# Three of eight groups of X per layer scaled on ScalarE and turned plainly, LN sums with operands added on VectorE over more units, V products 256 wide

## The chip, the core and the metric

The kernel runs on one core of one Trainium2 chip, and the metric is the time of that core in microseconds. The core has TensorE (PE, matmul; its weight loads are PEld), VectorE (DVE), ScalarE (ACT), GpSimd (POOL) and SyncE (SP), which here only issues transfers. Each engine carries out its own list of instructions in order; they meet through semaphores.

## The reference

One block of attention and MLP (first block, one layer) and then two layers of a second block, on 256 tokens of width 2048, all in float32. Cut to what the change touches:

```python
def one_block(args):                       # first block, attention, 16 heads of 128
    ...
    a = jnp.where(mask, jnp.exp(log_beta + suffix), 0.0)
    return jnp.einsum('bhqk,bhkd->bhqd', a.astype(v.dtype), v)      # the V products
...
for l in range(DEPTH_2):                   # second block, two layers
    h = rms_norm_2(x, norm_g[l]) * (1.0 + scale) + shift
    z = h @ w_in[l]                        # 2048 x 4928
    ...                                    # attention (mla), and beside it:
    u = causal_depthwise_conv(u, dw_w[l], dw_b[l])                  # 31 taps, 1024 channels
    u = jax.nn.silu(layer_norm(u, conv_ln_g[l], conv_ln_b[l]))      # mean and variance over channels
    u = u @ w_pw[l] + b_pw[l]
    conv_out = u * jax.nn.silu(conv_gate)
    y = jnp.concatenate([mla_out, conv_out], axis=-1) @ w_out[l]
    x = x + gate * y
```

## The kernel before

All products with weights are cut into units. A unit is a block of weights of 128 x 1024 numbers (one transfer of 512 KB) and the matmuls that use it: for each of two blocks of 128 weight rows and each of two tiles `t` of 128 tokens, three matmuls 512 wide (high part times high, high times low, low times high of a float32 split in two), 12 in all. `after[n]` lists the small tasks of step `n`. Each engine walks over the steps and carries out its part of the tasks of `after[n]`; TensorE does it behind unit `n`, ScalarE and VectorE do it ahead of the weights of that step. ScalarE makes the high part `WH` of a unit's weights (`high`, L1187), VectorE the low part `WL` (L1218); a step of both normally prepares the unit four further on, and ScalarE waits there until the unit four back has left its buffer. TensorE starts a unit when `WL` of it is written. So a task that comes late on VectorE holds up everything that stands behind it in its list.

I call the first unit of a layer's product with `w_in` z0. Tasks that the change touches:

- **Start of a layer (`chain`, L288).** x is kept with tokens on the partitions, in X[128, t, 2048]; z needs it turned, with channels on the partitions, and scaled by 1/rms of the token. Per layer there are 8 groups of 4 blocks of 128 x 128, named (t, q). `h_turn` (L591) turns a group and scales it at once, by a float32 matmul of each block of X with a diagonal matrix DG that holds 1/rms. `h_shift` (ScalarE, L997) or `h_scale` (VectorE, L1387) then applies the column's factor and shift and writes FB, four instructions 128 wide a group; `h_split` rounds it to the high part on ScalarE (L984) and takes the low part on VectorE (L1218, `AHL<-FB,AHL`). Groups (0, 3), (1, 2), (1, 3) come last: TensorE turns them behind z0+1, z0+2 and z0+3. The first eight units need the groups one after another: z0+6 is the first that reads group (1, 3), in its fourth matmul, which waits for that low part (`rows`, L784).
- **V products (`sb_out`, L578).** For each of 16 heads three float32 matmuls 128 wide: V0 with two blocks of TA, and V1 with one.
- **Layer norm of the convolution (L385 on).** The convolution ends on VectorE at step z0+96. Then `ln_sum` adds channel tiles (VectorE), `ln_mean` sums over the partitions with a matrix of ones (TensorE, three float32 matmuls 256 wide, L667), `ln_centre` takes the mean off (VectorE), squares (ScalarE, L1122) and adds pairs of squares (VectorE, L1565, L1567), `ln_var` sums these over the partitions (TensorE, four float32 matmuls one column wide, L675), `ln_rstd` (VectorE and POOL), `ln_scale` multiplies (VectorE, L1578), and `ln_act` does four pairs cp of channel tiles: silu (ScalarE, L1129), high part ULH (ScalarE, L1133), low part ULL (VectorE, L1218, `ULL<-SQL,ULH`). These feed the product with `w_pw`, whose first unit is z0+108; unit z0+108+cp waits for ULL of pair cp.
- **`o_add` (L1604).** Between them stands the product with the upper half of `w_out`, units z0+92 to z0+107. Its column block c is added to x on VectorE by four instructions 512 wide (L1612, L1613, L1617 twice), in the lists of steps z0+95, z0+99, z0+103 and z0+107.

All of this is one list per engine written out in Python; there is no scheduler. `ln_act` of the last pair is put ahead of the other tasks of its step:

```python
for cp in range(4):
    after[s + 7 + cp].insert(0 if cp == 3 else len(after[s + 7 + cp]), ("ln_act", l, cp))   # s = z0 + 97
```

Of the kernel before, what the change touches and what calls it, by code (L numbers as in the profile page):

```python
# [9 lines left out]
ALU = mybir.AluOpType  # L10
# [70 lines left out]
def build(nc, A, out):  # L81
    ctx = ExitStack()
    with ctx:
# [97 lines left out]
        U1 = put("U1", [128, 2, 512], off=oBH + 4 * K)  # L181
        DG = put("DG", [128, 2, 128], off=oBH)
# [242 lines left out]
        for c in range(4):  # L425
# [33 lines left out]
        rope_zero = tally("rope_rows_cleared")  # L459
# [6 lines left out]
                   kr_sq, kr_ms, kr_rot, q_sq, q_ms, q_rstd, q_rot, rot, k_sq, k_ms, k_rs, k_nrm, k_rope, rope_zero, mx, ex, rcp, o_high, conv_d, x_mid, p_bias, p_gated,  # L466
# [8 lines left out]

        flat = lambda ap: ap.rearrange("p a b -> p (a b)")
# [15 lines left out]
        def tensor_program(e):  # L492
# [354 lines left out]
        def scalar_program(e):  # L847
# [333 lines left out]
            def high(n):  # L1181
# [3 lines left out]
                if n >= NH:  # L1185
# [4 lines left out]
                         sb_scores=sb_scores, sb_high=sb_high, sb_sums=sb_sums, sb_out=sb_out, hid_evict=hid_evict, hid_split=hid_split, h_split=h_split, h_first=h_first, h_shift=h_shift, x_end_square=x_end_square, high=high,  # L1190
# [22 lines left out]
        def vector_program(e):  # L1213
# [201 lines left out]
            def pads_(l):  # L1415
                e.wait_ge(*T.ready(("h", l, 7)))
# [132 lines left out]
            def ln_sum(l, part):  # L1549
                for ct in range(4 * part, 4 * part + 4):  # L1550
                    e.wait_ge(*conv_d.at(l, ct, 30))
                if part == 0:
                    over_tiles(FB[:, 2, 0:256], CA[:, 0:4, :]).then_inc(*ln_d.up(l, "sum", 0))
                else:
                    e.tensor_tensor(FB[:, 3, :], flat(CA[:, 4:6, :]), flat(CA[:, 6:8, :]), ALU.add).then_inc(*ln_d.up(l, "sum", 1))

            def ln_centre(l):
# [9 lines left out]
                e.tensor_tensor(SQL[:, 0, :], SQL[:, 0, :], SQL[:, 2, :], ALU.add).then_inc(*ln_d.up(l, "squares"))  # L1567
# [36 lines left out]
            def o_add(l, part, c):  # L1604
# [10 lines left out]
                for t in range(2):  # L1615
# [6 lines left out]
                         att_scores=att_scores, att_recip=att_recip, att_out=att_out, att_back=att_back, conv=conv, ln_sum=ln_sum, ln_centre=ln_centre,  # L1622
# [231 lines left out]
```

## Time and profile before

| | |
|---|---|
| median of three runs | 1913.95 us (1913.6 to 1915.55) |
| the profiled execution | 1914.18 us, of which the span of the trace is 1912.3 us |
| PE busy | 1905.0 us, 100% of the span, 9406 instructions |
| PEld | 1609.9 us, 84% |
| DVE | 1558.5 us, 81% |
| ACT | 1027.4 us, 54% |
| POOL | 137.0 us, 7% |
| granted TensorE clock | 1.000 over the span |
| moved by DMA | 445.22 MB, 233 GB/s |

Busy means that some instruction of the engine has its record open. Records of TensorE overlap: one 512 wide is some 390 ns long, while the next starts some 230 ns later. So a busy TensorE can still lose time, and what a matmul costs is the distance between starts (in the chain of waits, its share), not the length of its record. A float32 matmul has two records in the trace, a transpose one.

### The profile page before, as it was taken

The page shows a single profiled execution, that of the slowest core. Times are in us where ns is not written, and L with a number is a line of the kernel's source. Part 1 is how long each engine was busy: PE and PEld are TensorE (multiplying, and loading weights), DVE is VectorE, ACT ScalarE, POOL GpSimd, SP SyncE. Part 2 cuts the span into 40 slices and gives each one's busy share as a digit, 9 for nine tenths or more (in the row PEclk, how much of TensorE's full clock was granted, in tenths as well). Part 3 has the DMA queues.
Part 4 walks back from the last instruction along what each step waited for, and adds up shares of the span by engine and source line. Part 5 has one row for each costly group of instructions (what it writes and reads, how often), then busy time and mean ns, then how long its engine had stood idle before and what let it go on. Part 6 is the DMA issues. An engine that isn't in the chain of part 4 may idle for free.

```text
span 1912.3 us, 25289 instructions
## 1 busy us (share of the span) xinstructions
PE 1905.0 (100%) x9406; PEld 1609.9 (84%) x9406; DVE 1558.5 (81%) x2131; ACT 1027.4 (54%) x1509; POOL 137.0 (7%) x88
## 2 busy tenths in 40 slices
PE   9999999999999999999999999999999999999999
PEld 7888888888888888888888888888888888888887
DVE  5888888788888888888887568888898688888986
ACT  6646556454444444444445454567656555667562
POOL 1232233000000000000000000001100000010000
PEclk9999999999999999999999999999999999999999
DMA  7787877889898888888887546655556466555554
GB/s 260 248 273 252 295 248 247 272 277 313 285 302 286 294 302 284 303 296 296 284 305 253 182 154 188 192 162 166 162 188 198 144 193 177 172 168 160 200 186 143
DMA packets 259181, 445.22 MB, mean 233 GB/s; under 512 B 15883, under 2 KB 123421, under 8 KB 258803
## 3 DMA queue, kind: packets, MB, share of 16 engines
q1 hardware_dynamic: 258643, 443.42, 71.4%
q8 instruction: 75, 1.23, 0.3%
q14 instruction: 47, 0.39, 0.1%
q10 hardware_dynamic: 416, 0.19, 0.0%
HBM read 441.39 MB, written 2.16 MB: 232 GB/s over the span
## 4 chain that ended last, share of the span: by engine, by line
PE 99%; DVE 0%; ACT 0%; issue 0%; POOL 0%; ACTq 0%; DVEq 0%
PE P L741 72%; PE P L799 13%; PE P L800 6%; PE P L501 2%; PE P L595 1%; PE P L634 1%; PE P L633 1%; PE P L619 0%; PE P L561 0%; PE P L541 0%; PE P L540 0%; PE P L641 0%; PE P L726 0%; PE P L586 0%; PE P L587 0%; PE P L652 0%
## 5 line engine op out<-in xcount | busy, mean ns | idle before, releaser
L1218 DVE TENSOR_TENSOR WL<-RAW,WH 128x1024 fp32r<-128x1024 f32 (+1 forms) x649 | 790.4, 1223 | 233.9 <-ACT WH L1187 231.3
L1187 ACT ACTIVATE WH<-RAW 128x1024 fp32r<-128x1024 f32 (+1 forms) x647 | 669.8, 1046 | 520.3 <-PE P L741 252.3
L741 PE MATMUL P<-WH,AHL 128*128 128x512 f32 (+1 forms) x2048 | 642.6, 389 | 0.9 <-ACT WH L1187 0.6
L741 PEld LDWEIGHTS P<-WH,AHL 128*128 128x128 f32 x2048 | 382.1, 188 | 76.9 <-issue 1.9
L741 PE MATMUL P<-WL,AHL 128*128 128x512 f32 (+1 forms) x1024 | 392.1, 385 | 0.0
L799 PE MATMUL P<-AHL,WH 128*128 128x512 f32 x1024 | 359.9, 398 | 0.0
L741 PE MATMUL P<-WH,BH 128*128 128x512 f32 x896 | 351.4, 392 | 0.0
L741 PE MATMUL P<-WH,BL 128*128 128x512 f32 x896 | 349.0, 390 | 0.0
L741 PE MATMUL P<-WL,BH 128*128 128x512 f32 x896 | 348.8, 389 | 0.0
L800 PE MATMUL P<-AHL,WL 128*128 128x256 f32 x1024 | 282.3, 281 | 0.0
L1215 DVE SCALAR_TENSOR_TENSOR ADA<-RAW,CC,ADA 128x1024 f32<-128x1024 f32 x180 | 237.9, 1322 | 0.0
L799 PEld LDWEIGHTS P<-AHL,WH 128*128 128x128 f32 x1024 | 190.7, 188 | 44.2
L741 PEld LDWEIGHTS P<-WL,AHL 128*128 128x128 f32 x1024 | 192.4, 188 | 35.6 <-DVE WL L1218 0.4
L1215 DVE SCALAR_TENSOR_TENSOR CA<-UT,DW,CA 128x256 f32<-128x256 f32 x480 | 204.1, 476 | 0.0
L741 PEld LDWEIGHTS P<-WH,BL 128*128 128x128 f32 x896 | 168.2, 188 | 35.3
L741 PEld LDWEIGHTS P<-WL,BH 128*128 128x128 f32 x896 | 168.3, 188 | 34.4
L741 PEld LDWEIGHTS P<-WH,BH 128*128 128x128 f32 x896 | 168.2, 188 | 34.3
L800 PEld LDWEIGHTS P<-AHL,WL 128*128 128x128 f32 x1024 | 193.4, 189 | 3.1
L1662 POOL TENSOR_TENSOR ST<-ST,CST 128x4 f32<-128x4 f32 (+3 forms) x36 | 66.0, 1834 | 1504.2 <-DVE ST L1215 911.7
L1215 DVE SCALAR_TENSOR_TENSOR X<-P,ST,X 128x512 f32<-128x512 f32 x64 | 45.1, 746 | 6.9 <-PE P L741 6.7
L974 ACT ACTIVATE HID<-P 128x512 f32<-128x512 f32 x32 | 19.1, 597 | 46.8 <-PE P L799 46.8
L1366 DVE TENSOR_TENSOR HID<-P,HID 128x512 f32<-128x512 f32 x32 | 22.1, 691 | 24.1 <-ACT HID L974 24.1
(268 smaller groups left out, 1451.4 us busy)
## 6 DMA issues: line engine op xcount, KB each, us to landing
RAW<-in_ada_w_dram SPq DMA_DIRECT2D x192, 512.0 KB, 5.0
RAW<-in_mlp_w_in_dram SPq DMA_DIRECT2D x128, 512.0 KB, 4.8
RAW<-in_mlp_w_out_dram SPq DMA_DIRECT2D x128, 512.0 KB, 5.2
RAW<-in_sb_w_qkv_dram SPq DMA_DIRECT2D x95, 512.0 KB, 4.9
RAW<-in_w_in_dram SPq DMA_DIRECT2D x80, 512.0 KB, 4.0
RAW<-in_w_in_dram SPq DMA_DIRECT2D x128, 256.0 KB, 3.2
RAW<-in_w_out_dram SPq DMA_DIRECT2D x64, 512.0 KB, 4.3
RAW<-in_sb_w_o_dram SPq DMA_DIRECT2D x32, 512.0 KB, 5.3
```

The lines of the kernel that those rows point to most:

```text
L501: m = e.transpose(pb[:, (2 * i + t) * 128:(2 * i + t + 1) * 128], src[:, t, kt * 128:(kt + 1) * 128], IDN)
L595: m = e.matmul(pb[:, k * 128:(k + 1) * 128], X[:, t, (4 * q + k) * 128:(4 * q + k + 1) * 128], DG[:, t, :], start=True, stop=True)
L633: e.matmul(pb[:, o:o + n], TT[:, 0, qs], TT[:, 1, ks], start=True, stop=False)
L634: m = e.matmul(pb[:, o:o + n], TT[:, 2, t * 128:(t + 1) * 128], TT[:, 3, ks], start=False, stop=True)
L741: return e.matmul(P[:, 2 * u.pair + t, 0:u.w], x, w, start=u.first and k == 0 and part == 0, stop=u.last and k == u.nk - 1 and part == 2)
L799: both = lambda: e.matmul(o.rearrange("p (x n) -> p x n", x=2), WH[:, s, w], AHL[:, :, kt, :], start=u.first and k == 0, stop=last, skip_g ...
L800: lower = lambda: e.matmul(o[:, 0:256], WL[:, s, w], AH[:, kt, :], start=False, stop=False, skip_group_check=True)
L1187: e.activation(WH[:, n % NH, 0:size], RAW[:, i % NR, 0:size], ACT.Copy).then_inc(w_high, 1)
L1215: return e.scalar_tensor_tensor(out=o, in0=x, scalar=s, in1=y, op0=op0, op1=op1)
L1218: return e.tensor_tensor(o, x, h.bitcast(F32), ALU.subtract)
L1366: e.tensor_tensor(v, P[:, p:p + 2, 0:256], HID[:, c % 2, :, :], ALU.add).then_inc(pair_emptied[opened["m1", c][0]], 1)
L1662: return e.tensor_tensor(o, x, MH.to_broadcast([128, n]), ALU.pow)
```

## The change

X of groups (0, 3), (1, 2) and (1, 3) is multiplied by 1/rms on ScalarE into a new tile XS, as task `x_scale` at the head of steps z0, z0+1 and z0+2, and TensorE turns XS with plain transposes. After `ln_sum` VectorE adds the three operands of the mean to one in two more instructions, so that `ln_mean` is one matmul; the adding of squares is a task of its own, `ln_pairs`, one step later and with one instruction more, so that `ln_var` is two matmuls; `ln_var`, `ln_rstd`, `ln_scale` and `ln_act` come one step later. In the V products V0 meets both blocks of TA in one matmul 256 wide.

```diff
+        XS = put("XS", [128, 3, 512], off=oS)
...
-            after[b] += [("h_split", l, 1, 1)]
-            after[b + 1] += [("h_shift", l, 0, 2), ("h_split", l, 0, 2), ("h_turn", l, 0, 3)]
-            after[b + 2] += [("h_turn", l, 1, 2), ("h_shift", l, 0, 3), ("h_split", l, 1, 2)]
+            after[b] += [("x_scale", l, 0, 3), ("h_split", l, 1, 1)]
+            after[b + 1] += [("x_scale", l, 1, 2), ("h_shift", l, 0, 2), ("h_split", l, 0, 2), ("h_turn", l, 0, 3)]
+            after[b + 2] += [("x_scale", l, 1, 3), ("h_turn", l, 1, 2), ("h_shift", l, 0, 3), ("h_split", l, 1, 2)]
...
-            after[s + 5].append(("ln_var", l))
-            after[s + 5].insert(0, ("ln_rstd", l))
-            after[s + 7].append(("ln_scale", l))
+            after[s + 3].append(("ln_pairs", l))
+            after[s + 6].append(("ln_var", l))
+            after[s + 6].insert(0, ("ln_rstd", l))
+            after[s + 8].append(("ln_scale", l))
             for cp in range(4):
-                after[s + 7 + cp].insert(0 if cp == 3 else len(after[s + 7 + cp]), ("ln_act", l, cp))
+                after[s + 8 + cp].insert(0 if cp == 3 else len(after[s + 8 + cp]), ("ln_act", l, cp))
...
-                    e.matmul(o[:, 0:128], v0, TA[:, h, 0:128], start=True, stop=True)
-                    e.matmul(o[:, 128:256], v0, TA[:, h, 128:256], start=True, stop=False)
-                    m = e.matmul(o[:, 128:256], v1, TA[:, h, 256:384], start=False, stop=True)
+                    e.matmul(o, v0, TA[:, h, 0:256], start=True, stop=False, skip_group_check=True)
+                    m = e.matmul(o[:, 128:256], v1, TA[:, h, 256:384], start=False, stop=True, skip_group_check=True)
...
             def h_turn(l, t, q):
                 pb = bank(("h", l, t, q))
+                if (t, q) in scaled_slot:
+                    e.wait_ge(*x_scaled.at(l, t, q))
+                    for k in range(4):
+                        m = e.transpose(pb[:, k * 128:(k + 1) * 128], XS[:, scaled_slot[t, q], k * 128:(k + 1) * 128], IDN)
+                    m.then_inc(*T.filled(("h", l, t, q)))
+                    return
...
             def ln_mean(l):
                 pb = bank(("lnm", l))
-                for part in range(2):
-                    e.wait_ge(*ln_d.at(l, "sum", part))
-                for i, x in enumerate((FB[:, 2, 0:256], FB[:, 3, 0:256], FB[:, 3, 256:512])):
-                    m = e.matmul(pb[:, 0:256], ONE, x, start=i == 0, stop=i == 2)
+                e.wait_ge(*ln_d.at(l, "sum", 3))
+                e.matmul(pb[:, 0:256], ONE, FB[:, 2, 0:256], start=True, stop=True).then_inc(*T.filled(("lnm", l)))
...
-                for part in range(2):
-                    for t in range(2):
-                        m = e.matmul(pb[:, t:t + 1], SQL[:, 0, part * 256 + t * 128:part * 256 + (t + 1) * 128], ONE[:, 0:1],
+                for t in range(2):
+                    m = e.matmul(pb[:, t:t + 1], SQL[:, 0, t * 128:(t + 1) * 128], ONE[:, 0:1], start=t == 0, stop=t == 1, skip_group_check=True)
...
+            def x_scale(l, t, q):
+                e.wait_ge(*rstd.at(("ob", 0) if l else ("m2", 7), t))
+                e.activation(XS[:, scaled_slot[t, q], :], X[:, t, 512 * q:512 * q + 512], ACT.Copy, scale=ST[:, 74 + t:75 + t]).then_inc(*x_scaled.up(l, t, q))
...
+                    e.tensor_tensor(FB[:, 2, 0:256], FB[:, 2, 0:256], FB[:, 3, 0:256], ALU.add).then_inc(*ln_d.up(l, "sum", 2))
+                    e.wait_ge(*ln_d.at(l, "sum", 2))
+                    e.tensor_tensor(FB[:, 2, 0:256], FB[:, 2, 0:256], FB[:, 3, 256:512], ALU.add).then_inc(*ln_d.up(l, "sum", 3))
...
+            def ln_pairs(l):
                 for i in range(2):
                     e.wait_ge(*ln_a.at(l, 2 * i + 1))
                     e.tensor_tensor(SQL[:, 2 * i, :], SQL[:, 2 * i, :], SQL[:, 2 * i + 1, :], ALU.add).then_inc(*ln_d.up(l, "pair", i))
                 e.wait_ge(*ln_d.at(l, "pair", 1))
-                e.tensor_tensor(SQL[:, 0, :], SQL[:, 0, :], SQL[:, 2, :], ALU.add).then_inc(*ln_d.up(l, "squares"))
+                e.tensor_tensor(SQL[:, 0, :], SQL[:, 0, :], SQL[:, 2, :], ALU.add).then_inc(*ln_d.up(l, "quarter"))
+                e.wait_ge(*ln_d.at(l, "quarter"))
+                e.tensor_tensor(SQL[:, 0, 0:256], SQL[:, 0, 0:256], SQL[:, 0, 256:512], ALU.add).then_inc(*ln_d.up(l, "squares"))
```

`pads` (VectorE, L1416) now waits for the turning of group (1, 3). The lists of the engines move at these places.

On ScalarE, steps z0-1 to z0+3 of layer 0, before (AHL is the high part of a group, FB the shifted group, WH the weights):

```order
L997 ACTIVATE FB<-P,MOD,SCL 128x128 x4
L984 ACTIVATE AHL<-FB 128x4x128
L1187 ACTIVATE WH<-RAW 128x1024
L997 ACTIVATE FB<-P,MOD,SCL 128x128 x4
L984 ACTIVATE AHL<-FB 128x4x128
L1187 ACTIVATE WH<-RAW 128x1024
L997 ACTIVATE FB<-P,MOD,SCL 128x128 x4
L984 ACTIVATE AHL<-FB 128x4x128
L1187 ACTIVATE WH<-RAW 128x1024 x2
```

and in the changed kernel:

```order
L1004 ACTIVATE FB<-P,MOD,SCL 128x128 x4
L995 ACTIVATE XS<-X,ST 128x512
L987 ACTIVATE AHL<-FB 128x4x128
L1194 ACTIVATE WH<-RAW 128x1024
L995 ACTIVATE XS<-X,ST 128x512
L1004 ACTIVATE FB<-P,MOD,SCL 128x128 x4
L987 ACTIVATE AHL<-FB 128x4x128
L1194 ACTIVATE WH<-RAW 128x1024
L995 ACTIVATE XS<-X,ST 128x512
L1004 ACTIVATE FB<-P,MOD,SCL 128x128 x4
L987 ACTIVATE AHL<-FB 128x4x128
L1194 ACTIVATE WH<-RAW 128x1024 x2
```

Nothing is taken out here; two XS now stand ahead of the second WH (that of z0+4), and a third ahead of the last group.

On VectorE, steps z0+97 to z0+103 of layer 0, before (CA is the convolution's result, SQL the squares, G the gate row of `o_add`):

```order
L1555 TENSOR_TENSOR FB<-CA 128x512
L1218 TENSOR_TENSOR WL<-RAW,WH 128x1024 x2
L1612 TENSOR_TENSOR FB<-P,G 128x512
L1613 TENSOR_TENSOR FB<-P,G 128x512
L1617 TENSOR_TENSOR X<-X,FB 128x512 x2
L1215 SCALAR_TENSOR_TENSOR CA<-P,CA 128x1024 x2
L1565 TENSOR_TENSOR SQL<-SQL 128x512 x2
L1567 TENSOR_TENSOR SQL<-SQL 128x512
L1218 TENSOR_TENSOR WL<-RAW,WH 128x1024 x3
L1571 TENSOR_SCALAR ST<-P 128x2
```

and in the changed kernel, from the centring (CA) on:

```order
L1222 SCALAR_TENSOR_TENSOR CA<-P,CA 128x1024 x2
L1225 TENSOR_TENSOR WL<-RAW,WH 128x1024
L1579 TENSOR_TENSOR SQL<-SQL 128x512 x2
L1581 TENSOR_TENSOR SQL<-SQL 128x512
L1583 TENSOR_TENSOR SQL<-SQL 128x256
L1225 TENSOR_TENSOR WL<-RAW,WH 128x1024 x3
L1587 TENSOR_SCALAR ST<-P 128x2
L1628 TENSOR_TENSOR FB<-P,G 128x512
```

One WL is now ahead of the sums of squares, there is a fourth sum, and the WL that stood behind the small L1571 is now ahead of its counterpart L1587. Two instructions 128x256 also follow the counterpart of L1555.

On VectorE, steps z0+105 to z0+108, where ULL is the low part of a pair, before:

```order
L1218 TENSOR_TENSOR ULL<-SQL,ULH 128x512
L1218 TENSOR_TENSOR WL<-RAW,WH 128x1024
L1218 TENSOR_TENSOR ULL<-SQL,ULH 128x512
L1218 TENSOR_TENSOR WL<-RAW,WH 128x1024
L1218 TENSOR_TENSOR ULL<-SQL,ULH 128x512
L1612 TENSOR_TENSOR FB<-P,G 128x512
L1613 TENSOR_TENSOR FB<-P,G 128x512
L1617 TENSOR_TENSOR X<-X,FB 128x512 x2
L1218 TENSOR_TENSOR WL<-RAW,WH 128x1024 x4
```

and in the changed kernel:

```order
L1225 TENSOR_TENSOR ULL<-SQL,ULH 128x512
L1225 TENSOR_TENSOR WL<-RAW,WH 128x1024
L1628 TENSOR_TENSOR FB<-P,G 128x512
L1629 TENSOR_TENSOR FB<-P,G 128x512
L1633 TENSOR_TENSOR X<-X,FB 128x512 x2
L1225 TENSOR_TENSOR ULL<-SQL,ULH 128x512
L1225 TENSOR_TENSOR WL<-RAW,WH 128x1024
L1225 TENSOR_TENSOR ULL<-SQL,ULH 128x512
L1225 TENSOR_TENSOR WL<-RAW,WH 128x1024 x3
```

The first ULL in both lists is that of pair 1. The four instructions of `o_add` stood behind the ULL of pair 3; now they stand ahead of the ULL of pair 2.

## Rows read from the trace of the kernel before

**Rows 1.** The page's chain that ended last: shares by engine.

```profile
PE 99%; DVE 0%; ACT 0%; issue 0%; POOL 0%; ACTq 0%; DVEq 0%
```

**Rows 2.** Groups of TensorE by form: busy us, mean ns of one record.

```profile
L595 PE MATMUL P<-DG,X 128*128 128x128 f32 x128 | 16.4, 276 | 1.1 <-DVE DG L1384 1.0
L501 PE MATMUL P<-CST,U 128*128 128x128 f32 x64 | 8.3, 272 | 0.0
```

**Rows 3.** The chain of waits in order of time: start us, us, what, records.

```profile
108.06 0.22 PE P L586 x2
...
1133.12 0.89 PE P L595 x8
...
1137.67 2.75 PE P L741 x12
...
1204.88 0.44 PE P L501 x4
...
1424.81 1.29 PE P L667 x6
...
1434.29 0.79 PE P L675 x8
```

**Rows 4.** Timeline of ScalarE, start of layer 0: start us, us, what, [idle before].

```profile
1136.51 0.63 ACT L984 ACTIVATE AHL<-FB 128x512 fp32r<-128x512 f32 x1
1137.05 1.04 ACT L1187 ACTIVATE WH<-RAW 128x1024 fp32r<-128x1024 f32 x1
1137.99 1.49 ACT L997 ACTIVATE FB<-P,MOD,SCL 128x128 f32<-128x128 f32 x4
...
1140.05 1.04 ACT L1187 ACTIVATE WH<-RAW 128x1024 fp32r<-128x1024 f32 x1
...
1143.66 0.63 ACT L984 ACTIVATE AHL<-FB 128x512 fp32r<-128x512 f32 x1 [1.18 <-DVE FB L1387]
```

**Rows 5.** Timeline of VectorE, start of layer 0.

```profile
1141.13 1.22 DVE L1218 TENSOR_TENSOR WL<-RAW,WH 128x1024 fp32r<-128x1024 f32 x1 [0.25 <-ACT WH L1187]
...
1150.22 0.69 DVE L1218 TENSOR_TENSOR AHL<-FB,AHL 128x512 fp32r<-128x512 f32 x1 [0.70 <-ACT AHL L984]
```

**Rows 6.** Timeline of TensorE, both layers, around the fourth matmul of z0+6.

```profile
1150.01 0.62 PE L741 MATMUL P<-WH,AHL 128*128 128x512 f32 x2
...
1150.68 0.78 PE L741 MATMUL P<-WH,AHL 128*128 128x512 f32 x2
...
1542.14 0.84 PE L741 MATMUL P<-WH,AHL 128*128 128x512 f32 x2
```

**Rows 7.** Timeline of ScalarE, first attention: a 512 wide pass read from PSUM.

```profile
111.83 0.69 ACT L918 ACTIVATE QK<-P,ST 128x512 f32<-128x512 f32 x1
```

**Rows 8.** Timeline of VectorE, layer norm of layer 0.

```profile
1424.94 0.69 DVE L1612 TENSOR_TENSOR FB<-P,G 128x512 f32<-128x512 f32 x1 [0.38 <-PE P L741]
...
1427.48 2.35 DVE L1215 SCALAR_TENSOR_TENSOR CA<-P,CA 128x1024 f32<-128x1024 f32 x2
...
1432.38 3.49 DVE L1218 TENSOR_TENSOR WL<-RAW,WH 128x1024 fp32r<-128x1024 f32 x3
1435.79 0.15 DVE L1571 TENSOR_SCALAR ST<-P 128x2 f32<-128x2 f32 x1
...
1441.77 2.34 DVE L1578 TENSOR_TENSOR CA<-CA,P 128x1024 f32<-128x1024 f32 x2
...
1450.18 0.69 DVE L1218 TENSOR_TENSOR ULL<-SQL,ULH 128x512 fp32r<-128x512 f32 x1 [0.48 <-ACT ULH L1133]
```

**Rows 9.** The same view of layer 1, ahead of its second `o_add`.

```profile
1814.80 1.22 DVE L1218 TENSOR_TENSOR WL<-RAW,WH 128x1024 fp32r<-128x1024 f32 x1 [0.32 <-ACT WH L1187]
1816.46 0.69 DVE L1612 TENSOR_TENSOR FB<-P,G 128x512 f32<-128x512 f32 x1 [0.44 <-PE P L741]
```

**Rows 10.** Timeline of ScalarE, layer norm of layer 0: WH after the squares.

```profile
1430.92 2.94 ACT L1187 ACTIVATE WH<-RAW 128x1024 fp32r<-128x1024 f32 x3
```

**Rows 11.** Timeline of TensorE: the first matmul of z0+105, layer 0.

```profile
1440.88 0.48 PE L741 MATMUL P<-WH,BH 128*128 128x512 f32 x1
```

More of the change, by code:

```diff
@@ L458, in build @@
         k_sq, k_ms, k_rs, k_nrm, k_rope = tally("k_squares"), tally("k_mean"), tally("k_rstd"), tally("k_scale"), tally("k_rope")
-        rope_zero = tally("rope_rows_cleared")
+        rope_zero, x_scaled = tally("rope_rows_cleared"), tally("x_scaled")
         mx, ex, rcp, o_high = tally("score_max"), tally("score_exp"), tally("score_recip"), tally("o_high")
@@ L465, in build @@
                    lnexp, tn_mask, a_exp, a_mask, bh_high, rstd_sq, hid_part, hid_sq, hid_high, hid_low, pads, tabs, sig, lat_sq, lat_ms, lat_r, lat_high,
-                   kr_sq, kr_ms, kr_rot, q_sq, q_ms, q_rstd, q_rot, rot, k_sq, k_ms, k_rs, k_nrm, k_rope, rope_zero, mx, ex, rcp, o_high, conv_d, x_mid, p_bias, p_gated,
+                   kr_sq, kr_ms, kr_rot, q_sq, q_ms, q_rstd, q_rot, rot, k_sq, k_ms, k_rs, k_nrm, k_rope, rope_zero, x_scaled, mx, ex, rcp, o_high, conv_d, x_mid, p_bias, p_gated,
                    ln_d, ln_a, ln_p, ul_high, ul_low, gact, p_high, x_done]
@@ L474, in psum @@
             return P[:, 2 * opened[g, c][0] + t, 0:w]
+        scaled_slot = {(0, 3): 0, (1, 2): 1, (1, 3): 2}
         flat = lambda ap: ap.rearrange("p a b -> p (a b)")
@@ L663, in ln_mean @@
                 pb = bank(("lnm", l))
-                for part in range(2):
-                    e.wait_ge(*ln_d.at(l, "sum", part))
-                for i, x in enumerate((FB[:, 2, 0:256], FB[:, 3, 0:256], FB[:, 3, 256:512])):
-                    m = e.matmul(pb[:, 0:256], ONE, x, start=i == 0, stop=i == 2)
-                m.then_inc(*T.filled(("lnm", l)))
+                e.wait_ge(*ln_d.at(l, "sum", 3))
+                e.matmul(pb[:, 0:256], ONE, FB[:, 2, 0:256], start=True, stop=True).then_inc(*T.filled(("lnm", l)))
             def ln_var(l):
@@ L672, in ln_var @@
                 e.wait_ge(*ln_d.at(l, "squares"))
-                for part in range(2):
-                    for t in range(2):
-                        m = e.matmul(pb[:, t:t + 1], SQL[:, 0, part * 256 + t * 128:part * 256 + (t + 1) * 128], ONE[:, 0:1],
-                                     start=part == 0 and t == 0, stop=part == 1 and t == 1, skip_group_check=True)
+                for t in range(2):
+                    m = e.matmul(pb[:, t:t + 1], SQL[:, 0, t * 128:(t + 1) * 128], ONE[:, 0:1], start=t == 0, stop=t == 1, skip_group_check=True)
                 m.then_inc(*T.filled(("lnv", l)))
@@ L1189, in scalar_program @@
             tasks = dict(x_turn=x_turn, x_square=x_square, columns=columns, angles=angles, qk_evict=qk_evict, v_evict=v_evict, qk_turn=qk_turn,
-                         sb_scores=sb_scores, sb_high=sb_high, sb_sums=sb_sums, sb_out=sb_out, hid_evict=hid_evict, hid_split=hid_split, h_split=h_split, h_first=h_first, h_shift=h_shift, x_end_square=x_end_square, high=high,
+                         sb_scores=sb_scores, sb_high=sb_high, sb_sums=sb_sums, sb_out=sb_out, hid_evict=hid_evict, hid_split=hid_split, h_split=h_split, h_first=h_first, x_scale=x_scale, h_shift=h_shift, x_end_square=x_end_square, high=high,
                          z_evict=z_evict, glu=glu, lat_turn=lat_turn, q_evict=q_evict, k_evict=k_evict, k_scale=k_scale, att_turn=att_turn, att_scores=att_scores,
@@ L1415, in pads_ @@
             def pads_(l):
-                e.wait_ge(*T.ready(("h", l, 7)))
+                e.wait_ge(*T.ready(("h", l, 1, 3)))
                 e.memset(UT[:, :, 0:30], 0.0).then_inc(*pads.up(l))
@@ L1555, in ln_sum @@
                     e.tensor_tensor(FB[:, 3, :], flat(CA[:, 4:6, :]), flat(CA[:, 6:8, :]), ALU.add).then_inc(*ln_d.up(l, "sum", 1))
+                    e.wait_ge(*ln_d.at(l, "sum", 0))
+                    e.wait_ge(*ln_d.at(l, "sum", 1))
+                    e.tensor_tensor(FB[:, 2, 0:256], FB[:, 2, 0:256], FB[:, 3, 0:256], ALU.add).then_inc(*ln_d.up(l, "sum", 2))
+                    e.wait_ge(*ln_d.at(l, "sum", 2))
+                    e.tensor_tensor(FB[:, 2, 0:256], FB[:, 2, 0:256], FB[:, 3, 256:512], ALU.add).then_inc(*ln_d.up(l, "sum", 3))
             def ln_centre(l):
@@ L1621, in vector_program @@
                          glu=glu, z_evict=z_evict, lat_turn=lat_turn, q_rope=q_rope, k_rstd=k_rstd, k_scale=k_scale,
-                         att_scores=att_scores, att_recip=att_recip, att_out=att_out, att_back=att_back, conv=conv, ln_sum=ln_sum, ln_centre=ln_centre,
+                         att_scores=att_scores, att_recip=att_recip, att_out=att_out, att_back=att_back, conv=conv, ln_sum=ln_sum, ln_centre=ln_centre, ln_pairs=ln_pairs,
                          ln_rstd=ln_rstd, ln_scale=ln_scale, ln_act=ln_act, p_evict=p_evict, p_turn=p_turn, o_add=o_add)
```

## The prediction

> **What bounds the kernel now.** I read the chain that ended last first: TensorE holds 99% of it [rows 1]. The obvious conclusion is that whatever is taken off TensorE comes off the time. Next I read the price of each kind of matmul there. A record is 270 to 280 ns long [rows 2], but records overlap; the chain gives the distance between starts [rows 3]: a record of a float32 matmul 128 wide takes 0.111 us (8 in 0.89, 2 in 0.22), one 256 wide 0.215 (6 in 1.29), one column wide 0.099 (8 in 0.79), a transpose 0.11 (4 in 0.44), a matmul of a unit 0.229 (12 in 2.75), so a unit 2.75.
>
> Then I looked, in the timelines of the places that the change touches, for the engines that feed TensorE, since TensorE's 99% hides short waits. There is one in each layer. At the fourth matmul of z0+6 two matmuls take 0.78 and 0.84 instead of 0.62 [rows 6], a wait of 0.16 and 0.22. The low part of group (1, 3) is written from 1150.22 for 0.69, to 1150.91 [rows 5]; the second of the two matmuls starts at 1150.68 + 0.78 - 0.39 = 1151.07 (0.39 is a record: 0.62 less the distance 0.23). So TensorE arrives there early, and starts 0.16 behind the write. The start of each layer is set by ScalarE and VectorE.
>
> **The change, turning.** TensorE turns six groups for 0.44 instead of 0.89: 6 x 0.45 = 2.7 us off TensorE, 1.35 a layer. But these lie ahead of z0+6, where it waits already; they count for nothing as long as that low part is no earlier. It will be later. ScalarE goes without a gap from 1136.51: high part of (1, 1), WH of z0+3 at 1137.05, shift at 1137.99, WH of z0+4 at 1140.05 [rows 4]. VectorE's WL of z0+4 at 1141.13 waits for that WH [rows 5], which ends at 1141.09: a handing over costs 0.04. Behind this WL stand, each waiting for the one before it, VectorE's factor and shift for (1, 2), its high part at 1143.66 on ScalarE, which had waited 1.18 for it [rows 4], the WH and WL of z0+5 and z0+6, the same for (1, 3), and the write at 1150.22. Two of the three new passes stand ahead of the WH at 1140.05. The third falls into the 1.18.
>
> What a pass costs: the trace has no such pass; the nearest is the high part at 1136.51, 512 wide from SBUF to SBUF, which takes 0.54 to the next start [rows 4]. The lower bound is half of a 1024 wide pass, (1137.99 - 1137.05) / 2 = 0.47 [rows 4], the upper one 0.76, a record of 0.69 from PSUM [rows 7] and a wait of 0.07. I take 0.54. Two passes on the path of each layer: **+1.08 a layer, +2.16 in all**, 1.9 to 3.0. TensorE will lose its 1.35 there too: with the old 0.16 it waits some 2.6 us a layer. Part of it shows early: XS of (0, 3) is ready at about 1136.51 + 0.63 = 1137.14, while TensorE comes to this turning at 1137.67 - 0.89 = 1136.78 [rows 3, 4]; everything from z0+2 on is queued behind. Behind z0+6 all three engines are later by the same amount, so later slack stays.
>
> What the skill says speaks against it too. Transposes and float32 matmuls have the same records (272 and 276 ns) and about the same distances, 0.11 [rows 2, 3]. The Trainium skill (TensorE: Matmul & The Clock Gate, Part 4: PE-mode transpose) gives a transpose about 275 ns within a kernel. The record agrees; taken as its price, 24 transposes would be 6.6 us against the 5.3 that go, where the distances give 2.6. The sum here is the same by both, since TensorE waits at z0+6 anyway.
>
> **V products.** Per head six records of 0.111, 0.666, become two of 0.215 and two of 0.111, 0.652. 16 heads: **-0.2** [rows 3]. It is real, since TensorE does not wait there, but it is nothing: the price goes by columns, and these are the same. Bounds 0 and -0.4 (if a second weight load less gave 0.01 more).
>
> **Layer norm, TensorE's part.** Four of six records 256 wide go, 0.86, and four of eight one column wide, 0.40: 1.26 a layer [rows 3], 2.5 in all. Again the question is who arrives last, at z0+110 this time.
>
> **Layer norm, VectorE's part**, in the clock of layer 0 before. TensorE starts z0+105 at 1440.88 [rows 11], and z0+110 5 x 2.75 later, at 1454.63. The ULL of pair 2 that it needs is written from 1450.18 to 1450.87 [rows 8]: slack 3.6. Now the list is followed from the first instruction of `o_add`, 1424.94. Centring starts at 1427.48 (so `o_add` takes 2.54) and squares and WH follow as before; this WH, of z0+103, ends at 1430.92 + 1.04 = 1431.96 [rows 4, 10]. Its WL now comes first, at 1432.00; a WL takes 1.14, as (1435.79 - 1432.38) / 3 shows [rows 8], so the sums begin at 1433.14. A 512 wide sum is a record of 0.69 [rows 8], less 0.08 of overlap if the next waits for nothing, plus 0.04 if it waits; the three take 0.61 + 0.73 + 0.73. One 256 wide is not in these rows; from 0.69 for 512 and 1.22 for 1024 [rows 5, 8] I estimate 0.43, 0.35 to the next start. That is 1435.56. Three WL, 3.41, the small rstd instruction, 0.07, `o_add`, 2.54, two WL, 2.28: `ln_scale` begins at 1443.86, 2.09 later than its 1441.77 [rows 8]. The pairs follow 2.09 later, and pair 2 would be at 1452.27. But it now stands behind the last `o_add`: 2.54 more, of which the 0.48 that VectorE had waited there [rows 8] and the 0.08 are taken up: +1.98, 1454.25. End 1454.94, and TensorE starts z0+110 at 1455.10, **0.47 later than before**. TensorE alone would have been there at 1453.4; it waits 1.7 at this place or in part before it (WL of z0+103 ends at 1433.2, about when TensorE now needs it). Pair 3, behind it, has a whole unit of slack.
>
> In layer 0 the two added instructions behind `ln_sum`, 2 x (0.43 + 0.04) = 0.94, begin this list late: VectorE had 0.38 + 0.08 free ahead of that `o_add` [rows 8], so 0.48 remain, and layer 0 gets 0.47 + 0.48 = 0.95. In layer 1 it had 0.32 + 0.44 + 2 x 0.08 = 0.92 free [rows 9], and nothing remains: 0.47. **Layer norm: +1.4.** Bounds: below -2.5, if VectorE comes in time in both layers; above +2.4, if each of some 12 handings over in a layer takes 0.04 more.
>
> **Sum.** 2.16 - 0.2 + 1.4 = +3.3 on the profiled execution, 1914.18 to 1917.5; the median of the runs is 0.2 below it, so 1913.95 becomes **1917.3**, +0.17%. A difference under 0.2%, 3.8 us, is about what a measurement of this kernel cannot tell from none; so this is "no change", near its edge.
>
> **Rivals.**
> *A, TensorE bounds everything.* The 99% [rows 1] speak for it. All that is removed counts: 2.7 + 0.2 + 2.5 = 5.4, 1908.5. Against it are the waits of rows 6: it needs ScalarE to be earlier, and ScalarE gets more work. 6%.
> *B, the start of a layer as forecast, the layer norm gains.* 2.16 - 0.2 - 2.5 = -0.5, 1913.4. For it: TensorE had 3.6 of slack there. Against: I find 2.09 + 1.98 + 1.26 = 5.3 taken out of the 3.6, so my list would have to be wrong by 1.7 us of VectorE's time. 20%; one layer alone would lie between.
> *C, slower.* The scaling passes on ScalarE cost more than the high part. Four stand on the path; from 0.67 each on (0.54 + a quarter of the 0.5 that lack to 3.8) the kernel is measurably slower, and at the upper bound of 0.76 the sum is +4.2, 1918.1. For it: a pass with a factor read from SBUF in rows 7 is 0.69. Against: that one reads PSUM, in a crowded stretch. 27%.
> The Trainium skill (ScalarE: Activation LUTs, Rules for kernel authors) budgets 0.3 us and 0.83 ns per element, 0.72 for such a pass. The high part's distance of 0.54 [rows 4] disagrees with it; by the page the sum would be +4.1, which is C.
>
> **How the numbers follow.** Forecast 47%, A 6%, B 20%, C 27%. A fifth of the forecast's own spread lies over +3.8, and a small part of C under it. Faster 0.07, same 0.60, slower 0.33. The range 1912 to 1920 holds the forecast, B and C; below it is A, above it a layer norm at its upper bound together with C.
>
> **What would show it.** In the changed kernel's trace the XS passes have 0.5 to 0.6 to the next start; the low part of (1, 3) is written 1.1 later than before, counted from the start of the layer, and TensorE waits there and at the turnings some 2.6 a layer. In the layer norm the ULL of pair 2 comes behind `o_add`, and TensorE waits for it by 1 to 1.7 in both layers. V takes 2.6 instead of 2.7 us for four heads. I am wrong if TensorE shows no wait at z0+110 (B), if z0+6 starts earlier than before (A), or if an XS pass holds ScalarE for 0.67 or more (C).

## The result and the profile after

The changed kernel takes **1917.52 us** (median of 13 runs, 1916.58 to 1919.39), the kernel before, timed beside it, 1913.94 (1913.43 to 1915.55): a ratio of 1.0019, 95% interval 1.0012 to 1.0026. It is slower by 3.6 us, 0.19%, where 1917.3 was forecast: just under the 0.2% below which the prediction speaks of no change, and the interval reaches over it. The interval lies above 1 as a whole. The profiled execution spans 1915.4, 3.1 more than before, at a granted clock of 1.000.

The page's part on the chain that ended last, and TensorE's waits (us in total, times, longest) in the changed kernel:

```profile
PE 90%; DVE 6%; ACT 2%; issue 1%; POOL 0%; ACTq 0%; DVEq 0%
```

```profile
PE P L744 <- DVE AHL L1225: 2.3, 4, 1.0
PE P L744 <- DVE ULL L1225: 1.9, 2, 1.0
...
PE P L598 <- ACT XS L995: 1.0, 2, 0.5
...
PE P L744 <- DVE WL L1225: 0.5, 2, 0.3
```

The 99% of [rows 1] has become 90%: the chain now leaves TensorE at the places where it waits. None of these four lines has a counterpart in that view of the kernel before, for which its waits of 0.16 and 0.22 [rows 6] are too short. Two are at the start of a layer (AHL, XS), two in the layer norm (ULL, WL).

**Start of layer 0.** ScalarE, then the last low part of VectorE, then TensorE (start us, us, what, [idle before]); before: [rows 4 to 6].

```profile
1134.82 1.48 ACT L1004 ACTIVATE FB<-P,MOD,SCL 128x128 f32<-128x128 f32 x4
1136.19 0.73 ACT L995 ACTIVATE XS<-X,ST 128x512 f32<-128x512 f32 x1
1136.81 0.63 ACT L987 ACTIVATE AHL<-FB 128x512 fp32r<-128x512 f32 x1
1137.33 1.06 ACT L1194 ACTIVATE WH<-RAW 128x1024 fp32r<-128x1024 f32 x1
1138.27 0.72 ACT L995 ACTIVATE XS<-X,ST 128x512 f32<-128x512 f32 x1
1138.89 1.50 ACT L1004 ACTIVATE FB<-P,MOD,SCL 128x128 f32<-128x128 f32 x4
```

```profile
1151.12 0.69 DVE L1225 TENSOR_TENSOR AHL<-FB,AHL 128x512 fp32r<-128x512 f32 x1 [0.70 <-ACT AHL L987]
```

```profile
1136.21 0.39 PE L744 MATMUL P<-WH,AHL 128*128 128x512 f32 x1
1137.06 0.63 PE L598 MATMUL P<-CST,XS 128*128 128x128 f32 x4 [0.47 <-ACT XS L995]
...
1144.60 0.40 PE L744 MATMUL P<-WH,AHL 128*128 128x512 f32 x1
1145.99 0.50 PE L744 MATMUL P<-WH,AHL 128*128 128x512 f32 x1 [0.99 <-DVE AHL L1225]
...
1151.33 0.39 PE L744 MATMUL P<-WH,AHL 128*128 128x512 f32 x1
1151.87 0.50 PE L744 MATMUL P<-WH,AHL 128*128 128x512 f32 x1 [0.15 <-DVE AHL L1225]
```

A scaling pass holds ScalarE for 0.62 (1136.81 - 1136.19, 1138.89 - 1138.27); its record is 0.72. TensorE's three shown waits are at the turning of (0, 3), at the fourth matmul of z0+4 and at that of z0+6. Where the undisturbed distance is 0.23, its starts are 0.85, 1.39 and 0.54 apart there: waits of 0.62, 1.16 and 0.31.

**Layer norm of layer 0**, VectorE and then TensorE; before: [rows 8, 11].

```profile
1425.95 0.68 DVE L1628 TENSOR_TENSOR FB<-P,G 128x512 f32<-128x512 f32 x1
...
1444.80 2.35 DVE L1594 TENSOR_TENSOR CA<-CA,P 128x1024 f32<-128x1024 f32 x2
...
1452.65 0.68 DVE L1628 TENSOR_TENSOR FB<-P,G 128x512 f32<-128x512 f32 x1
1453.25 0.68 DVE L1629 TENSOR_TENSOR FB<-P,G 128x512 f32<-128x512 f32 x1
1453.97 1.29 DVE L1633 TENSOR_TENSOR X<-X,FB 128x512 f32<-128x512 f32 x2
1455.18 0.68 DVE L1225 TENSOR_TENSOR ULL<-SQL,ULH 128x512 fp32r<-128x512 f32 x1
```

```profile
1454.59 0.39 PE L744 MATMUL P<-WH,ULL 128*128 128x512 f32 x1
1455.92 0.50 PE L744 MATMUL P<-WH,ULH 128*128 128x512 f32 x1 [0.95 <-DVE ULL L1225]
```

The ULL of pair 2 stands right behind `o_add`, and TensorE waits 1.33 - 0.22 = 1.11 for it (starts are 0.22 to 0.23 apart here).

**A ledger by stretches.** The time up to the first layer differs by up to 1.3 us between profiles of kernels that have the same code there, so spans are not subtracted. Marks, each the start of a row: D, VectorE writes the diagonal of tile 0 (`DG`); L, the last low part 512 wide of the layer's start; T, TensorE's first transposes of p (`P<-CST,MP`); then the end of the span. In us:

| kernel | D to L | L to T | T to D | D to L | L to T | T to end | sum |
|---|---|---|---|---|---|---|---|
| before | 24.48 | 312.66 | 54.30 | 24.55 | 312.69 | 57.88 | 786.56 |
| changed | 25.54 | 313.10 | 54.30 | 25.89 | 313.07 | 57.92 | 789.82 |
| e1 turning only | 25.56 | 312.65 | 54.30 | 25.65 | 312.65 | 57.88 | 788.69 |
| e2 norm only | 24.48 | 313.11 | 54.30 | 24.81 | 313.10 | 57.89 | 787.69 |
| e3 V only | 24.45 | 312.67 | 54.29 | 24.57 | 312.67 | 57.99 | 786.64 |
| e4 | 25.55 | 312.66 | 54.29 | 25.91 | 312.77 | 57.89 | 789.07 |
| e5 | 24.47 | 313.03 | 54.30 | 24.83 | 313.12 | 57.96 | 787.71 |
| e6 | 24.47 | 313.13 | 54.29 | 24.83 | 313.25 | 57.94 | 787.91 |
| e7 | 24.46 | 312.69 | 54.29 | 24.83 | 312.75 | 57.96 | 786.98 |
| e8 | 24.46 | 312.80 | 54.33 | 24.83 | 312.84 | 57.94 | 787.20 |
| e9 | 22.40 | 313.73 | 54.33 | 22.74 | 313.77 | 57.94 | 784.91 |
| e10 | 22.09 | 314.77 | 54.29 | 22.21 | 314.78 | 57.95 | 786.09 |
| e11 | 24.46 | 312.73 | 54.29 | 24.54 | 312.69 | 57.90 | 786.61 |
| e12 | 24.47 | 312.69 | 54.29 | 24.82 | 312.67 | 57.94 | 786.88 |

Changed less before: +1.06, +0.44, 0, +1.34, +0.38, sum +3.26. Rows that nothing touches agree to about 0.1. In e9 and e10 VectorE writes the last two low parts one right behind the other and the trace view joins them in one row, so their L is some 0.7 early; for these two only the sum of D to L and L to T can be compared.

### The profile page after: what moved, and what is told of

Read it like the earlier page. It is cut to its first block, busy times and chain, and to the rows that moved or that the text cites. A ratio compares the mean times of both kernels' runs of the same rounds, so it can differ in the third digit from the quotient of the medians.

```text
span 1915.4 us, 25159 instructions
## 1 busy us (share of the span) xinstructions
PE 1902.3 (99%) x9334; PEld 1603.0 (84%) x9334; DVE 1559.8 (81%) x2137; ACT 1030.3 (54%) x1515; POOL 134.6 (7%) x88
## 3 DMA queue, kind: packets, MB, share of 16 engines
HBM read 441.39 MB, written 2.16 MB: 232 GB/s over the span
## 4 chain that ended last, share of the span: by engine, by line
PE 90%; DVE 6%; ACT 2%; issue 1%; POOL 0%; ACTq 0%; DVEq 0%
PE P L744 64%; PE P L802 12%; PE P L803 6%; DVE WL L1225 2%; PE P L504 2%; DVE CA L1222 1%; ACT WH L1194 1%; DVE X L1633 1%; PE P L642 1%; PE P L641 1%; DVE FB L1394 0%; PE P L603 0%; PE P L627 0%; DVE FB L1628 0%; PE P L589 0%
```

## The experiments

Medians are of 11 runs each. The kernel before, beside them, had 1913.72 (e1 to e4), 1913.96 (e5 to e7), 1914.19 (e8 to e11); e12 is a single run.

**e1 to e3, each part alone.** The kernel before with one part of the diff.

> The kernel before with the scaled turning alone (V products and layer norm as before). My theory, two scaling passes in ScalarE's list on the path of each layer, 2 x 0.54 a layer: +2.2 us. Rival A, TensorE bounds everything: 2.7 us less. If a pass costs 0.62, as its distance to the next start in the changed kernel reads, without anything else taken up: +2.5.

> The kernel before with the layer norm part alone. The prediction's term is +1.4 (0.95 in layer 0, 0.47 in layer 1). My reading of the changed kernel's trace is that 0.48 of layer 0 was one late transfer of G in one profiled execution: then 0.45 + 0.42, +0.9. Rival B, VectorE's list in time at z0+110: -2.5.

> The kernel before with the V products 256 wide alone. Price by columns: -0.2. Rival, each of the 16 matmuls and weight loads that go is worth a record's distance: up to -1.8 (16 x 0.11).

Measured: turning 1916.17, +2.45, ratio 1.0013 (1.0004 to 1.0022), ledger +2.13; norm 1914.76, +1.04, ratio 1.0005 (0.9996 to 1.0014), ledger +1.13; V 1913.56, -0.16, ratio 0.9999 (0.9990 to 1.0007). The intervals of norm and V hold 1, so these two rest on the ledger and the rows. The sum is +3.33, the whole +3.58; in the ledger 2.13 + 1.13 + 0.08 = 3.34 against 3.26: no interaction of the parts shows. Rival A (-2.7 for the turning) and rival B (-2.5 for the norm) are out. The V rows, here of the changed kernel, agree with the price by columns, 0.65 a head (107.72 to 108.37) where six records took 6 x 0.111 = 0.67 [rows 3]:

```profile
107.72 0.59 PE L589 MATMUL P<-TA,V 128*128 128x256 f32 x2
108.15 0.38 PE L590 MATMUL P<-TA,V 128*128 128x128 f32 x2
108.37 0.60 PE L589 MATMUL P<-TA,V 128*128 128x256 f32 x2
```

**e4, the ULL of pair 2 ahead of the last `o_add`.**

```diff
-                after[s + 8 + cp].insert(0 if cp == 3 else len(after[s + 8 + cp]), ("ln_act", l, cp))
+                after[s + 8 + cp].insert(0 if cp >= 2 else len(after[s + 8 + cp]), ("ln_act", l, cp))
```

> The changed kernel, with the ULL of pair 2 ahead of the last o_add on VectorE instead of behind it. My theory: the 1.98 of o_add go from the list, TensorE's wait at z0+110 (about 1.7 a layer) goes, and it is bound by its own chain there: 1.3 to 1.7 a layer less than the changed kernel, -2.6 to -3.4 in all, so about 1914.5. Rival: ln_scale later by a unit decides by itself, or pair 3 or the o_add becomes late: no change against the changed kernel.

Measured: 1916.45, 1.07 less than the changed kernel, not 2.6 to 3.4. The wait went to the next operand. VectorE and TensorE of e4:

```profile
1453.86 0.68 DVE L1628 TENSOR_TENSOR FB<-P,G 128x512 f32<-128x512 f32 x1
...
1456.38 1.22 DVE L1225 TENSOR_TENSOR WL<-RAW,WH 128x1024 fp32r<-128x1024 f32 x1
1457.52 0.69 DVE L1225 TENSOR_TENSOR ULL<-SQL,ULH 128x512 fp32r<-128x512 f32 x1
```

```profile
1457.35 0.39 PE L744 MATMUL P<-WH,ULL 128*128 128x512 f32 x1
1458.26 0.50 PE L744 MATMUL P<-WH,ULH 128*128 128x512 f32 x1 [0.53 <-DVE ULL L1225]
```

Pair 3 now stands behind `o_add` and a WL: a wait of 0.91 - 0.22 = 0.69 instead of 1.11, so 0.42 a layer; the ledger's two L to T give 0.44 and 0.30. My rival holds in part: pair 3 became late, though by less than pair 2 had been.

**e5, the scaling passes in ScalarE's idle stretches; e6, no scaling passes.** In e5:

```diff
-            after[b] += [("x_scale", l, 0, 3), ("h_split", l, 1, 1)]
+            after[b] += [("h_split", l, 1, 1)]
```

and likewise (0, 3) to the end of `after[b - 1]`'s turnings, (1, 2) ahead of `h_begin` of (1, 1), (1, 3) behind the shift of (0, 3). In e6 the three `x_scale` are taken out of the lists, and:

```diff
-                    e.wait_ge(*x_scaled.at(l, t, q))
+                    e.wait_ge(*h_diag.at(l, t))
...
-                        m = e.transpose(pb[:, k * 128:(k + 1) * 128], XS[:, scaled_slot[t, q], k * 128:(k + 1) * 128], IDN)
+                        m = e.transpose(pb[:, k * 128:(k + 1) * 128], X[:, t, (4 * q + k) * 128:(4 * q + k + 1) * 128], IDN)
```

> The changed kernel with its three scaling passes moved into ScalarE's idle stretches (the first ahead of the high parts of (0, 0), the second ahead of the halves of (1, 1), the third behind the shift of (0, 3)). My theory, only their place in ScalarE's list costs: 2.2 less than the changed kernel, and TensorE's turning saves nothing, so about 1915.3. Rival, the passes cost their time wherever they stand: no change. Rival A once more, TensorE's 2.7 count as soon as ScalarE is free: 4.9 less.

> The changed kernel without the three scaling passes; the groups (0, 3), (1, 2) and (1, 3) are turned by transposes of X itself. It leaves out the factor 1/rms of these groups. My theory: 2.2 less than the changed kernel, for TensorE's 1.35 a layer is lost in the wait at z0+6. Rival A: 2.7 more than that, 4.9 less.

Measured: 1914.86 and 1914.89, 2.66 and 2.63 less than the changed kernel; by the ledger 2.11 and 1.91. The first D to L is 24.47 in both, as before the change to 0.01, with three passes in idle time or none, and with 1.35 less work for TensorE. So the passes cost only by their place in ScalarE's list, and the turning saves nothing. ScalarE in e5, the pass in a stretch that was idle:

```profile
1131.93 0.42 ACT L987 ACTIVATE AHL<-FB 128x256 fp32r<-128x256 f32 x1 [0.68 <-DVE FB L1394]
1132.25 0.71 ACT L995 ACTIVATE XS<-X,ST 128x512 f32<-128x512 f32 x1
1133.48 0.94 ACT L987 ACTIVATE AHL<-FB 128x256 fp32r<-128x256 f32 x2 [0.52 <-DVE FB L1394]
```

**e7, e4 and e5 together; e8, that `o_add` one step later still**, behind pair 3:

```diff
+            late_add = [x for x in after[s + 10] if x[0] == "o_add"]
+            assert len(late_add) == 1
+            after[s + 10].remove(late_add[0])
+            after[s + 11].append(late_add[0])
```

> The scaling passes early and the ULL of pair 2 ahead of o_add, in one kernel. My theory, the two add up: about 5 less than the changed kernel, 1912.5, about 1.5 less than the kernel before: the layer norm gains 2 x 0.5 to 1.2, V 0.2, the turning nothing. Rival, the places share their slack: only one of the two counts, 1914 to 1915.

> The kernel of e7 (scaling early, ULL of pair 2 ahead of o_add), with this o_add moved one step later, behind the ULL of pair 3. In e4 and e7 TensorE waits 0.69 in each layer for the ULL of pair 3, which stands behind o_add and a WL. My theory, one list, one displaced wait: 1.2 to 1.4 less than e7, about 1913.0. Rival, the sums on VectorE delay something else in any case, or the unit that needs the PSUM pair of o_add waits now: no change against e7's 1914.35.

Measured: e7 1914.35 (ratio 1.0002, 0.9994 to 1.0011), no gain on the kernel before, and 3.2 less than the changed kernel where I expected 5. The ledger has both effects, e5's at each D to L and e4's at each L to T; what failed is the gain of the layer norm that I had put at 0.5 to 1.2 a layer. Its L to T, 312.69 and 312.75, is that of the kernel before: the 1.26 a layer that TensorE has less to do goes into waits. e8 1914.75 (ratio 1.0003), no better: my theory failed a second time, for a third wait took its place. TensorE of e8, at the first transposes of p:

```profile
1461.64 0.39 PE L748 MATMUL P<-WH,ULL 128*128 128x512 f32 x1
1462.66 0.63 PE L508 MATMUL P<-CST,MP 128*128 128x128 f32 x4 [0.63 <-DVE MP L1617]
```

VectorE's list, full from `o_add` on, now reaches the eviction of p late. At each of the three places tried for the 2.54 us of `o_add`, TensorE waits for something behind it.

**e9 and e10, the list that holds TensorE at the start of a layer made shorter.** e9 is e8, e10 the kernel before, each with this edit: the factor and shift leave VectorE's `h_split` for a function of their own, which stands earlier.

```diff
-                if on_vector(t, q):
-                    e.wait_ge(*T.ready(name))
-                    for j in range(4):
-                        m = h_scale(l, f, 4 * q + j, name, j)
-                    m.then_inc(*T.drained(name))
...
+            def h_fill(l, t, q):
+                name, f = ("h", l, t, q), FB[:, buffer(t, q), :]
+                e.wait_ge(*T.ready(name))
+                for j in range(4):
+                    m = h_scale(l, f, 4 * q + j, name, j)
+                m.then_inc(*T.drained(name))
...
-            after[b + 1] += [("h_shift", l, 0, 2), ("h_split", l, 0, 2), ("h_turn", l, 0, 3)]
+            after[b + 1] += [("h_shift", l, 0, 2), ("h_split", l, 0, 2), ("h_turn", l, 0, 3), ("h_fill", l, 1, 2)]
...
-            after[b + 3] += [("h_split", l, 0, 3), ("h_turn", l, 1, 3), ("h_split", l, 1, 3)]
+            after[b + 3] += [("h_fill", l, 1, 3), ("h_split", l, 0, 3), ("h_turn", l, 1, 3), ("h_split", l, 1, 3)]
```

> The kernel of e8, with VectorE's factor and shift of (1, 2) ahead of the WL of z0+4 instead of behind it, and those of (1, 3) ahead of the low part of (0, 3). This shortens the list that holds TensorE at the start of a layer (0.47 at z0+4 and 0.16 at z0+6 in e5). My theory: now the 1.35 a layer that the turning saves begin to count: 0.6 to 1.0 a layer less than e8, about 1911.4. Rival, the start of a layer is bound by something else, such as the weights: no change.

> The kernel before with that same reordering of the factors alone, and the turning by products with the diagonal. TensorE's whole wait there is 0.16 + 0.22, a further 0.23 at the second unit: 0.2 to 0.4 a layer less than before, about 1913.3. If by contrast the list alone decides, not TensorE, it gains as much as e9 gains over e8.

Measured: e9 **1912.34** (1911.86 to 1913.17), ratio to before 0.9991 (0.9982 to 0.9999); e10 1913.50, ratio 0.9997 (0.9988 to 1.0006). From D to T, e9 gains 1.13 and 1.16 on e8 (337.26 to 336.13, 337.67 to 336.51), a little more than the 0.6 to 1.0 I expected; e10 gains 0.28 and 0.25 on before (337.14 to 336.86, 337.24 to 336.99), within the 0.2 to 0.4. By the sums of the ledger these are 2.29 and 0.47, for the same reordering. I read the difference, 1.8, as the part of TensorE's turning time (2 x 1.35) that counts once the list is out of its way. No run isolates it. The rest goes in part into delays too short for the view of waits: in e9 two starts from 1137.29 on take 0.70 instead of 0.46. The XS line had gone with e5 and the ULL line with e8; now the AHL line, 1.3 in e8, is gone from e9's waits too:

```profile
PE P L508 <- DVE MP L1619: 1.2, 2, 0.6
PE P L733 <- DVE FB L1671: 1.2, 1, 1.2
PE P L607 <- DVE DG L1395: 1.0, 1, 1.0
PE P L748 <- ACT WH L1198: 0.6, 1, 0.6
PE P L748 <- DVE WL L1229: 0.5, 2, 0.3
```

Its median lies 1.85 under that of the kernel before. That is 0.1%, less than the 0.2% that a measurement tells from none, and the interval leaves 1 out only just.

**e11 and e12, three and four more instructions on VectorE, in the kernel before.** The second D to L is 24.81 to 24.83 against 24.55, +0.26 to +0.28, in e2, e5, e6, e7 and e8. All of them have the changed layer norm, which lies elsewhere, and no other cost at this place.

```diff
+                    for pad in range(3):
+                        e.memset(PADZ[:, 3 * l + pad:3 * l + pad + 1], 0.0)
```

> The kernel before with three memsets one column wide added to VectorE's list in each layer, behind the sum of the layer norm, so that every later instruction stands three places further, as with the change. All kernels with the changed layer norm show VectorE's factor of (1, 0) 0.35 later in layer 1, with nothing to wait for, and a packet of the instruction queue 0.6 behind it; the kernel before has such a packet behind a later instruction. My theory, VectorE's list is fetched in blocks and the boundary has moved by three places: +0.3 at that place in layer 1, the same as in the changed kernel, and the packet earlier by some 1.6. Rival, it is the layer norm's own work: nothing at that place, +0.1 in all.

> As e11, with four memsets in each layer instead of three, since the changed layer norm also adds a wait of its own ahead of one of its three instructions. In e11 the packet of the instruction queue came 0.6 behind the start of the second half of the factor of (1, 0), and that pair of instructions took 0.80 instead of 0.73. My theory, the boundary lies one place earlier now, right ahead of the first half, which has TensorE to wait for: it starts 0.35 later than in e11, as in the changed kernel, and the time from the diagonal of (0, .) of layer 1 to the low part of (1, 3) grows from 24.54 to about 24.83. Rival, the layer norm's own work: it stays at 24.5.

e11 (1913.94, ratio 0.9999) missed: 24.54. But the packet of the instruction queue, 8.4 behind D before (1525.60), came 7.1 behind D (1523.70), and the factor of (1, 0), two instructions, took 0.80. With a fourth memset e12 has 24.82, where 24.83 was expected. (Its time, one run of 1914.92 against 1913.59, says nothing here: its D alone comes 1.1 later than e11's.) That factor on VectorE in the changed kernel, in e11 and in e12:

```profile
1524.94 0.73 DVE L1394 TENSOR_SCALAR FB<-P,SCL,MOD 128x128 f32<-128x128 f32 x2 [1.20 <-PE P L603]
```

```profile
1522.65 0.80 DVE L1388 TENSOR_SCALAR FB<-P,SCL,MOD 128x128 f32<-128x128 f32 x2 [0.86 <-PE P L596]
```

```profile
1524.11 0.73 DVE L1388 TENSOR_SCALAR FB<-P,SCL,MOD 128x128 f32<-128x128 f32 x2 [1.22 <-PE P L596]
```

The packet in e12, in the DMA queues of the stretch 1524.9 to 1525.2 (packets, MB, share):

```profile
q14 instruction: 1, 0.01, 6.4%
```

The idle time, put down to TensorE, is 1.22 in e12 and 0.86 in e11, which differ by one memset some 100 us earlier. TensorE is not the cause: its turning of that group starts 4.92 behind D in both. The layer norm's own work is out as well, since e12 does not have it. That the change, with three instructions more a layer, behaves like four memsets and not like three is explained only by the guess in the expectation.

## Why the prediction was right, point by point

- **"The start of each layer is set by ScalarE and VectorE"**: right, and shown by e6, which has the shorter turning without the passes and the same 24.47.
- **"Two passes on the path", +1.08 a layer**: the first D to L is +1.06, e1 has +1.08 and +1.10. The price of one pass was mis-sized: 0.62 to the next start, not 0.54. It did not show, because the first pass starts 1.37 behind the shift's start (1136.19 - 1134.82), where before the high part of (1, 1) had come 1.52 behind it (1136.51 [rows 4] - 1134.99, the row of ScalarE ahead of it):

```profile
1134.99 1.48 ACT L997 ACTIVATE FB<-P,MOD,SCL 128x128 f32<-128x128 f32 x4
```

  The pass fills 0.15 of a wait: 2 x 0.62 - 0.15 = 1.09. That the two errors cancel to 0.01 is luck. The sign "0.5 to 0.6 to the next start" was passed by 0.02; C's condition, 0.67 or more, was not met. The 0.72 by the budget of the Trainium skill (ScalarE: Activation LUTs, Rules for kernel authors) is the length of the record, 0.71 to 0.73, and not the 0.62 that the list pays.
- **TensorE waits some 2.6 a layer there**: right in sum (0.62, 1.16, 0.31 above, and shorter delays at their restarts and in between, about 2.6 together), but most of it stands at z0+4's fourth matmul and at the turning of (0, 3), not at z0+6. The prediction has TensorE start 0.16 behind the write; in the changed kernel it starts 0.06 behind (1151.12 + 0.69 = 1151.81, then 1151.87), and the rest lies in the next start, 0.34 instead of 0.23 later.
- **V, -0.2**: -0.16, with rows of 0.65 a head; the time alone could not tell this from nothing.
- **Layer norm, layer 1, +0.47**: right, 0.38 in the ledger, 0.41 in e2. `ln_scale` begins 4.77 later (below, before and changed), of which 2.68 is what L is later (1544.41 against 1541.73), so 2.09, as forecast. The ULL of pair 2 comes behind `o_add`, and TensorE waits 1.1 for it as in layer 0.

```profile
1833.29 2.34 DVE L1578 TENSOR_TENSOR CA<-CA,P 128x1024 f32<-128x1024 f32 x2
```

```profile
1838.06 2.34 DVE L1594 TENSOR_TENSOR CA<-CA,P 128x1024 f32<-128x1024 f32 x2
```

- **Layer norm, layer 0, +0.95**: wrong by half, +0.44. `ln_scale` begins 1444.80 - 1441.77 = 3.03 later, of which 0.90 is what L is later, so 2.13, where 2.09 + 0.48 was forecast. The 0.48 for the two added instructions rested on [rows 8]'s 0.38 of free time ahead of that `o_add`. That was one execution's: in the profile before, VectorE had waited 0.38 for the gates' transfer 10 us earlier. VectorE of the kernel before there, then of e3, whose list is the same:

```profile
1414.83 0.69 DVE L1612 TENSOR_TENSOR FB<-P,G 128x512 f32<-128x512 f32 x1 [0.38 <-DMA G<-gates]
```

```profile
1422.68 1.23 DVE L1217 TENSOR_TENSOR WL<-RAW,WH 128x1024 fp32r<-128x1024 f32 x1 [0.31 <-ACT WH L1186]
1424.34 0.69 DVE L1611 TENSOR_TENSOR FB<-P,G 128x512 f32<-128x512 f32 x1 [0.44 <-PE P L740]
```

  In e3 it is idle for 0.31 and 0.44, as in layer 1 [rows 9], and so it is, to 0.01, in e1, e10 and e11, with no wait for the gates. e2, expected on this reading at 0.45 + 0.42, has 0.45 and 0.41 in its two L to T. A slack was read from a stretch that a late transfer had disturbed.
- **What was missed**: +0.28 at the start of layer 1, from the place of VectorE's instructions (e12); the prediction has no term for it. By the ledger: 2.16 forecast and 2.12 found for the passes, 1.4 forecast and 0.82 + 0.28 for the norm. The total came out as near as it did partly by luck: this stood in for half of the 0.5 of layer 0.
- **B was excluded by the wait at z0+110** and by e2 (+1.04, not -2.5), A by e1 (+2.45, not -2.7) and e6.

## What to carry to other kernels

An engine at 99% of the chain can still be the one that waits: compare the distances between its starts with those of an undisturbed piece, and look at which list ends last at each place; work taken off TensorE at the start of a layer counted for nothing until e9 shortened that list, and what the layer norm took off it counted in no kernel here. In a list without gaps, moving one item moves the wait to the next operand (pair 2, pair 3, then p), so price the whole list and not the item; and put added passes into idle stretches, where e5's cost nothing. Slack is to be read from both layers: where they differ, ask which transfer came late in the one execution that was profiled.

## What the runs showed of the hardware that was not expected

- The place of an instruction in VectorE's list has a price of its own. At the start of layer 1 one instruction starts late: by 0.09 in the kernel before (the one at 1524.90 comes 0.43 behind the start of the low part ahead of it, in the changed kernel, e11 and e12 0.34), by 0.07 in e11 (the second half of the factor of (1, 0)), by 0.35 in the changed kernel and in e12, where it is the first half, which also waits for TensorE. A packet of the instruction queue lands 0.7 behind it in the kernel before (1525.60), in e11 (1523.70) and in the changed kernel (1525.62), but 0.95 behind it in e12 (1525.06 behind 1524.11). Counted from D it lands after 8.4, 7.1, 7.1 and 7.4. So the late start is shown to depend on the count of instructions ahead of it, and the packet moves with that count; that both are one event, the list being fetched in blocks, is my reading, and the 0.95 does not fit it well. The Trainium skill (Advanced Engine Details and Errata, ISA Cache) has instructions cached in lines of 16 KB, 256 instructions. That goes with the reading, but the queue's 47 packets are 0.39 MB on the page of the changed kernel, 8.3 KB each, half of that.
- ScalarE's pass with a factor per partition, 512 wide from SBUF to SBUF, is 0.62 to the next start; the rounding pass of the same size 0.54 [rows 4].
